# Two attention loops of an fp32 two-block transformer: copies moved from DVE to ACT, weight conversions behind head copies, and an output tile one turn earlier

## The reference

```python
h = rmsnorm(x, n1); proj = h @ w_in
qa = axial_rope(rmsnorm(qa, q_norm), ...); ka = axial_rope(rmsnorm(ka, k_norm), ...)
ya = global_gqa(qa, ka, va)                      # 8 query heads, 2 key heads
yb = dilated_window_attention(qb, kb, vb)        # 8 heads, partial rope
y = concatenate([rmsnorm(ya, out_norm_a), rmsnorm(yb, out_norm_b)])
x = x + y @ w_out
u = square(relu(rmsnorm(x, n2) @ w_mlp_in)); x = x + u @ w_mlp_out
```

## Time and profile before

| | |
|---|---|
| timed runs | 2024.04 us median of 3 (2023.94 to 2024.36) |
| profiled execution | 2016.69 us, of which span 2014.9 us |
| mean granted TensorE clock | 0.973 |
| TensorE busy | 1870.3 us, 93% |
| DVE, ACT, POOL busy | 72%, 55%, 18% |
| chain that ended last | TensorE 78%, DVE 10%, ACT 5%, issue 4% |

### The profile page before, as it was taken

One profiled execution on the slowest core, in us unless ns is written; L12 is line 12 of the kernel. 1 busy time (PEld: TensorE's weight loads), 2 busy tenths in 40 slices (PEclk: granted clock), 3 DMA queues, 4 the chain that ended last, 5 costly groups with the idle time before them and its releaser, 6 DMA issues.

```text
span 2014.9 us, 26999 instructions
## 1 busy us (share of the span) xinstructions
PE 1870.3 (93%) x9005; PEld 1519.5 (75%) x9005; DVE 1457.9 (72%) x1677; ACT 1117.0 (55%) x1355; POOL 353.2 (18%) x292
## 2 busy tenths in 40 slices
PE   6889999979999997899989779999999999999995
PEld 5677886857888675688877558888888888888884
DVE  5548874455876676544467668989898989898985
ACT  5644443554443454444345446767677777777773
POOL 2722203443100463200045300000000000000000
PEclk9999999989999998899999889999999999999998
DMA  8328983417986341455453329999999999999992
GB/s 257 105 105 324 350 339 134 146 45 269 356 330 247 108 145 42 146 187 187 137 190 130 126 74 342 366 332 366 332 367 329 367 329 367 330 361 336 358 364 100
DMA packets 316453, 494.79 MB, mean 246 GB/s; under 512 B 22984, under 2 KB 238240, under 8 KB 310240
## 3 DMA queue, kind: packets, MB, share of 16 engines
q1 hardware_dynamic: 307584, 493.44, 70.8%
q10 hardware_dynamic: 8480, 0.13, 0.3%
q0 software_dynamic: 320, 0.36, 0.2%
HBM read 492.77 MB, written 1.10 MB: 245 GB/s over the span
## 4 chain that ended last, share of the span: by engine, by line
PE 78%; DVE 10%; ACT 5%; issue 4%; POOL 1%; DMA 1%; DVEq 0%; SPq 0%; POOLq 0%; ACTq 0%
PE bank L2088 23%; PE bank L2090 23%; PE bank L2089 23%; ACT w_hi L1700 2%; PE bank L2202 2%; ACT slab L1847 2%; PE bank L2550 2%; DVE w_lo L876 1%; DVE slab L1181 1%; PE bank L2293 1%; PE bank L2271 1%; PE bank L2508 1%; POOL w_lo L774 1%; DMA slab<-in_w_in 1%; DVE big L1622 1%
## 5 line engine op out<-in xcount | busy, mean ns | idle before, releaser
L876 DVE TENSOR_TENSOR w_lo<-slab,w_hi 128x2048 fp32r<-128x2048 f32 x371 | 855.0, 2308 | 232.6 <-ACT w_hi L1700 232.6
L1700 ACT ACTIVATE w_hi<-slab 128x2048 fp32r<-128x2048 f32 (+2 forms) x421 | 796.9, 1899 | 361.4 <-PE bank L2090 272.9
L2088 PE MATMUL bank<-w_hi,hT_hi 128*128 128x512 f32 (+3 forms) x1616 | 632.8, 392 | 16.4 <-DVE hT_lo L925 4.3
L2090 PE MATMUL bank<-w_hi,hT_lo 128*128 128x512 f32 (+3 forms) x1616 | 619.2, 383 | 0.0
L2089 PE MATMUL bank<-w_lo,hT_hi 128*128 128x512 f32 (+3 forms) x1616 | 618.8, 383 | 0.0
L2088 PEld LDWEIGHTS bank<-w_hi,hT_hi 128*128 128x128 f32 x1616 | 306.2, 189 | 75.0 <-DVE w_lo L876 9.1
L2090 PEld LDWEIGHTS bank<-w_hi,hT_lo 128*128 128x128 f32 x1616 | 305.9, 189 | 57.9
L2089 PEld LDWEIGHTS bank<-w_lo,hT_hi 128*128 128x128 f32 x1616 | 306.7, 190 | 52.5
L774 POOL TENSOR_TENSOR w_lo<-slab,w_hi 128x512 fp32r<-128x512 f32 (+2 forms) x200 | 254.9, 1309 | 397.2 <-ACT w_hi L1700 397.2
L2088 PE MATMUL bank<-w_hi,hid_hi 128*128 128x512 f32 x728 | 285.0, 391 | 6.2 <-DVE hid_lo L1449 6.2
L2090 PE MATMUL bank<-w_hi,hid_lo 128*128 128x512 f32 x728 | 284.3, 391 | 0.0
(11 more groups left out here) (224 smaller groups left out, 1337.9 us busy)
## 6 DMA issues: line engine op xcount, KB each, us to landing
slab<-in_w_exp_gate SPq DMA_DIRECT2D x176, 512.0 KB, 5.3
slab<-in_w_exp_up SPq DMA_DIRECT2D x176, 512.0 KB, 6.3
slab<-in_w_exp_down SPq DMA_DIRECT2D x176, 512.0 KB, 5.9
slab<-in_w_ada SPq DMA_DIRECT2D x48, 1024.0 KB, 5.0
slab<-in_w_mlp_in SPq DMA_DIRECT2D x64, 512.0 KB, 6.2
slab<-in_w_mlp_out SPq DMA_DIRECT2D x64, 512.0 KB, 6.2
slab<-in_w_in SPq DMA_DIRECT2D x56, 512.0 KB, 5.0
slab<-in_w_out SPq DMA_DIRECT2D x32, 512.0 KB, 4.6
```

What stands on the lines that cost most here:

```text
L876: dve.tensor_tensor(w_lo[:, q, 0:n], raw(s)[:, 0:n], w_hi[:, q, 0:n].bitcast(F32), ALU.subtract).then_inc(lo_dve, 1)
L1700: act.activation(w_hi[:, q, 0:n], raw(s)[:, 0:n], ACT.Copy).then_inc(hi_done, 1)
L2088: pe.matmul(dst, a_hi, b_hi, start=start, stop=False)
L2090: return pe.matmul(dst, a_lo, b_hi, start=False, stop=stop_)
```

## The change

Four edits, all for the first block (`l < DEPTH`); the second block's layers run through the same helpers with their old order.

1. For pairs 2 to 7 `second_out` is no longer on DVE but on ACT, right behind `first_out` and ahead of `y_high`.
2. In ACT's turn 2 the head copies `turned_out(4, 5, 6)` come ahead of the high parts of tiles 11 and 12.
3. TensorE does the second output tile in turn 8, between `values(6)` and `values(7)`, after the last `mx_done`, and into the score banks 0 and 1 instead of the banks PT. The products of turn 9 and the sum of squares follow each other directly. `add_part(1)` reads the score banks.
4. In DVE's turn 8 `add_part(0)` comes after `y_low(6)` instead of ahead of it.

```diff
--- before.py
+++ after.py
@@ -479,6 +479,10 @@
 
         def dup(t, o):
             return h[:, t, o:o + HD]
+
+        def both_by_act(l, u):
+
+            return l < DEPTH and u >= 2
 
         def y_square(u):
 
@@ -1266,37 +1270,37 @@
                                           ).then_inc(ms_done, 1)
                         roots[0] += 1
 
-                    def scaled(c, t, o):
+                    def scaled(c, t, o, banks):
                         at = x[:, t, c * COL:(c + 1) * COL]
-                        return dve.scalar_tensor_tensor(at, bank[(FA, PT)[c][t]][:, :], stat[:, 2, o + t:o + t + 1], at,
+                        return dve.scalar_tensor_tensor(at, bank[banks[c][t]][:, :], stat[:, 2, o + t:o + t + 1], at,
                                                         ALU.mult, ALU.add)
 
                     def add_part(c):
                         dve.wait_ge(w_used, FREE_SPLIT + T0 + tiles_in(l) + c + 1)
                         for t in range(TT):
-                            scaled(c, t, 2).then_inc(xp_done, 1)
+                            scaled(c, t, 2, (FA, SC)).then_inc(xp_done, 1)
 
                     def add_last(c, t):
                         if c and not t:
                             dve.wait_ge(part_done, PARTS * l + 1)
                         else:
                             dve.wait_ge(w_used, FREE_SPLIT + T0 + tiles_in(l) + 3 + c)
-                        updated(scaled(c, t, 4))
+                        updated(scaled(c, t, 4, (FA, PT)))
 
                     for n in range(NU + 2):
                         if n < NU:
                             masked_max(n)
                         if n == 6:
                             part_mean(2)
-                        if 0 <= n - 1 < NU:
+                        if 0 <= n - 1 < NU and not both_by_act(l, n - 1):
                             second_out(n - 1)
-                        if n == 8:
-                            dve.wait_ge(rstd_done, roots[0])
-                            add_part(0)
                         if n < NU:
                             normalise(n)
                         if 0 <= n - 2 < NU:
                             y_low(n - 2)
+                        if n == 8:
+                            dve.wait_ge(rstd_done, roots[0])
+                            add_part(0)
                         if n == 0:
                             query_rows()
                         if n == 1:
@@ -1853,6 +1857,11 @@
                     act.wait_ge(av_done, U0 + u)
                     act.activation(pt_set(0), bank[PT[0]][:, :], ACT.Copy).then_inc(pta_done, 1)
 
+                def second_out(u):
+
+                    act.wait_ge(ptb_t, pairs_before(l, u) + 1)
+                    act.activation(pt_set(1), bank[PT[1]][:, :], ACT.Copy).then_inc(ptb_done, 1)
+
                 def y_high(u):
 
                     k, half_ = y_chunk(l, u), bank[OB][:, (u % 2) * SEQ:(u % 2 + 1) * SEQ]
@@ -1880,6 +1889,8 @@
                             soft_exp(n)
                         if 0 <= n - 1 < NU:
                             first_out(n - 1)
+                            if both_by_act(l, n - 1):
+                                second_out(n - 1)
                         if 0 <= n - 2 < NU:
                             y_high(n - 2)
                         if n == 0:
@@ -1890,9 +1901,8 @@
                             hi_of(l, 10)
                             empty(VB1, COL, FA, 9)
                         if n == 2:
-                            hi_of(l, 11)
                             turned_out(4, 5, 6)
-                            hi_of(l, 12)
+                            hi_of(l, 11, 12)
                         if n == 8:
                             hi()
                         if n == 9:
@@ -2221,7 +2231,7 @@
                     turn_rows(ATT2_BANKS)
 
                 def banks_of(two):
-                    return [bank[b] for b in two]
+                    return [bank[b] for b in two[:TT]]
 
                 def in_tile(i, to, waits_rows=False):
 
@@ -2375,9 +2385,9 @@
                             pe.wait_ge(yl_done, PAIR0[l] + B1)
                             pe.wait_ge(ms_done, ROOT0[l] + 4)
                             out_tile(0, FA, True, True)
-                        if n == 9:
-                            out_tile(1, PT, True, True)
-                    pe.wait_ge(mx_done, 4 * (U0 + NU))
+                        if n == 8:
+                            pe.wait_ge(mx_done, 4 * (U0 + NU))
+                            out_tile(1, SC, True, True)
                     squares_sum(B1, SC[2])
                     pe.wait_ge(yl_done, PAIR0[l] + NU)
                     pe.wait_ge(xp_done, 2 * TT * l + TT)
```

## The result

The kernel after took 2011.19 us (median of 4 runs, 2008.17 to 2012.67), the kernel before 2024.01 us (4 runs, 2023.94 to 2024.36): a ratio of 0.9939 [0.9924, 0.9954], so it is 12.8 us (0.6%) faster where I had forecast 6.2, and the time lies below my range. Two more comparisons of the same two kernels, each on one chip in turn, gave 0.9962 [0.9947, 0.9977] both times (2014.27 against 2022.16 and 2013.16 against 2021.42 us, medians), which is 7.7 and 8.0 us. So two things need an explanation: why the best measured difference is some 8 us and not 6.2, and why the first comparison showed 12.8.

What follows compares the result with a forecast made beforehand. TensorE, busy 93% of the span, was taken as the bound, losing time at waits in the attention loops. Terms -5.89 - 1.47 + 1.2 = -6.2 us took 2024.0 to 2017.8 us, range 2014.0 to 2022.5.

Steps and rivals of the forecast that it cites:

- Part 1: Attention loops' ends: second output tile one turn forward removes TensorE's 2.67 us wait; gains 3.75 and 2.14, together 5.89 us.
- Part 3: ACT's turn 2: head copies ahead of weight parts; TensorE's later wait costs clock, +1.2 us, bounds 0 and +2.4.
- A fall is gone at 87.44, where it cost nothing that ended last in layer 0: Half clock after TensorE's 4.69 us wait for the first heads disappears, claimed to save nothing in layer 0.
- the exponentials at 91.0: Layer 0: pair 3's exponentials start at 91.0 as before, since ACT's work changes order, not sum; a well earlier start refutes.
- Part 2: Second score copy from DVE to ACT, six pairs a layer: +0.13 us layer 0, -1.60 layer 1, sum -1.47.
- first rival: More half clock: wait before first sum of squares grows 1.54 to 2.0 us, layer 0 falls too; 2022.2 us, chance 0.24.
- third rival: Less half clock: other spacing spares layer 1's 6.8 us stretch; 2015.5 us, or 2014.3; chance 0.12.
- The wait that I had expected at 4.4 us: TensorE waits for pair 3's normalised scores, before the transposes at 95.5; a 2.03 us wait becomes 4.4.
- nothing comes of it: Attention's gain is given back where the DMA sets the pace; time stays 2024 us, chance 0.07.
- slower: Half clock falls on product tiles all over four layers' attention loops; 2028 us, chance 0.07.

Runs made afterwards that it cites:

- tile_only: Kernel before with only the second output tile moved between the products of pairs 6 and 7 (edits 3 and 4): 2017.34 us, ratio 0.9976.
- heads_only: Kernel before with only the head copies put ahead of the weights' high parts on ACT in turn 2: 2016.97 us, ratio 0.9969.
- fill_turn2: Kernel before with 24 unread transposes in TensorE's 4.7 us wait in turn 2, ACT's order unchanged: 2017.53 us, ratio 0.9979.
- heads_split: Changed kernel with ACT's turn 2 as one head copy, weight 11's high part, two head copies, weight 12's high part: 2014.57 us, ratio 0.9955.
- no_heads: Changed kernel with the old ACT order in turn 2, a weight's high part ahead of the head copies: 2016.73 us, ratio 0.9962.
- no_copies: Changed kernel with the second score copy back on DVE: 2013.49 us, ratio 0.9956.
- squares_nocopy: Changed kernel with the first sum of squares in turn 6, the split head copies, and the second score copy back on DVE: 2011.76 us, ratio 0.9950.
- squares_split: Changed kernel with the first sum of squares in turn 6 and the late head copies split by a weight conversion: 2009.74 us, ratio 0.9944.
- fill_turn5: Changed kernel with 12 unread transposes in TensorE's wait before the first sum of squares: 2011.52 us, ratio 0.9956.
- squares_late: Changed kernel with the first sum of squares moved on TensorE from the end of turn 5 into turn 6: 2011.2 us, ratio 0.9941.

## Why the prediction was wrong, and where it was right

**Part 1 was right about its own stretch.** Forecast -5.89 us; from the first output tile to the third it is -5.3 us in the kernel after and -5.6 in tile_only, the new wait 0.48 us for 0.46. Every kernel with this edit has 16.6 to 16.9 us there, those without it 18.4 to 20.2: that is shown, and it is the largest term of the loops' 7.9 us. What it brings the whole kernel when it stands alone is less (2.6 us in the loops, -4.6 +- 1.9 in the runs), and its new wait was priced without a clock: in layer 1 the third tile behind it starts at half clock, and its first nine matmuls take 3.5 us where they took 2.2, 1.3 us that the forecast has at nothing. The third tile starts at 130.99 and 451.18 us, forecast 130.7 and 452.6; but the first of these hits by luck, for the loop starts 0.8 us earlier than before and loses 3.0 us in pair 6.

**Part 3 is the step that failed**: a loss of 1.2 us was forecast; heads_only takes -5.0 +- 2.4 us, and pairs 3 and 4 are 3.65 us shorter in it. It failed with the sentences "this part moves TensorE's wait instead of removing it" and "A fall is gone at 87.44, where it cost nothing that ended last in layer 0", and with the exponentials at 91.0. The order of ACT in layer 0's turn 2 and 3:

```profile
84.10 1.08 ACT L1842 ACTIVATE slab<-bank 128x512 f32<-128x512 f32 x2
...
84.84 0.63 PE L2249 MATMUL bank<-const,h 128*128 128x128 f32 x4 [2.90 <-ACT slab L1842]
...
85.50 0.60 ACT L1842 ACTIVATE slab<-bank 128x512 f32<-128x512 f32 x1 [0.32 <-PE bank L2249]
...
86.00 3.70 ACT L1704 ACTIVATE w_hi<-slab 128x2048 fp32r<-128x2048 f32 x2
...
89.60 0.50 ACT L1851 ACTIVATE slab<-slab,att 128x256 f32<-128x256 f32 x1
```

From the start of the first item to the exponentials it is 5.50 us, before 6.12 (84.91 to 91.03). I had taken ACT's work as a fixed sum "with the same short wait for the heads inside it". That wait was not fixed: 0.78 us before, since TensorE did the head transposes at half clock behind a wait of 4.69 us, and 0.32 us behind one of 2.90. The rows of the kernel before that stand between those of the earlier trace rows, and DVE's first maximum of pair 3:

```profile
88.56 0.60 ACT L1838 ACTIVATE slab<-bank 128x512 f32<-128x512 f32 x1 [0.78 <-PE bank L2239]
...
89.06 1.90 ACT L1700 ACTIVATE w_hi<-slab 128x2048 fp32r<-128x2048 f32 x1
...
90.57 0.42 DVE L1164 CUSTOM_DVE_ANT_0 slab<-bank,const 128x256 f32<-128x256 f32 x1 [4.04 <-PE bank L2253]
```

The other 0.17 us: before, the exponentials (91.03) started 1.97 us after the last conversion did (89.06); in fill_turn2 it is 1.80 (88.04 to 89.84), and here two conversions take 3.60 to that point. So before they also waited 0.17 us for a late maximum, which waited for the scores (90.57) and ended at 90.99. Pair 4 shows the same (5.51 and 6.72 to 4.92 and 4.61). I had priced a fall of the clock as something that this part adds; it was already paid for before, and the part took its cost away. Which of two things takes it away does not matter: with the heads first TensorE goes on 1.8 us earlier, counted from the loop's start, and still falls to half clock right behind the transposes, in heads_only too:

```profile
85.30:88.70 3.40, 3.40 (x18) 2.34 (x16) 1.47 (x8) 3.40 (x3) 3.40 (x4) 0.50 0.52 193
```

With the filling it starts as late as before, at full clock, and the pairs are as quick. The rival theory, that the gain needs the new order itself, fell with fill_turn2. That ACT's own sequence holds pairs 3 and 4 once TensorE is not late is argued, not shown; heads_split, which takes the wait of 0.32 us out of that sequence, fits it with 8.11. What the gain is worth beside the other parts is open: pairs 3 and 4 are 2.3 us shorter in the kernel after than in no_heads, the loops 1.8, and the runs show nothing of it (-7.7 both).

**Part 2 was counted partly on the same lateness.** Forecast -1.47. Of its -1.60 us in layer 1, 1.15 were the lateness of pair 3 in the earlier trace rows, which is half clock behind that same wait; part 3 removes it without any copy. Alone the copies are worth 0.6 us in the loops and -3.1 +- 1.6 in the time. Beside the other parts they shorten the loops by 1.5 us (no_copies against after) and by 1.4 (squares_nocopy against squares_split), near the forecast but at other places than the two it names: 1.0 of the 1.5 lies ahead of the first output tile. The runs can't show it: no_copies -10.2 +- 2.2 against -7.7 and -8.0 for the whole change, squares_nocopy 1.2 +- 2.3 us slower than squares_split. What they are worth in time stays open.

**The first rival was right about its place and did not decide.** The wait before the first sum of squares grew to 2.02 us, and the clock fell in layer 0 too:

```profile
93.74 1.09 PE L2281 MATMUL bank<-const,slab 128*128 128x128 f32 x8 [2.48 <-DVE slab L1185]
...
102.12 0.36 ACT L1870 ACTIVATE big<-bank 128x256 f32<-128x256 f32 x1
...
102.54 3.57 PE L2314 MATMUL bank<-const,big 128*128 128x1 f32 x16 [2.02 <-ACT big L1870]
...
106.04 2.08 PE L2263 MATMUL bank<-slab 64*128 64x256 f32 x8
```

Sixteen matmuls of one column took 3.57 us instead of 1.95, the scores behind them 2.08 instead of 1.14, and pair 6 took 3.0 us more (9.49 for 6.45); I had said 3.2. But layer 1 got 1.0 of it back (7.17 for 8.13): half clock lies on 3.4 us there (426.80, window above) instead of 6.8. So the third rival, "less half clock", was half right as well. The wait that I had expected at 4.4 us (pair 3's transposes) is the 2.48 us ahead of 93.74 there, and full clock followed it (1.00 from 93.80). The Trainium skill ("TensorE: Matmul & The Clock Gate", HAM oscillation) tells of a kernel whose bursts of matmuls, with waits of some 3 to 5 us between them, start at half rate every time. The prediction left the length of those waits out. The waits here are shorter and have no one outcome: behind that of 2.02 us the clock was 0.50, behind that of 2.90 us the first transposes still ran at full clock (0.63 us) and half clock came after them, and behind that of 2.48 us it was 1.00. The rivals "nothing comes of it" and "slower" did not come: the kernel after's mean is below before's in all three comparisons.

**The size of the miss.** The loops gave 7.9 us. After them some is paid back: the kernel after has a half-clock stretch at 157.10 at the start of layer 0's feed-forward that before does not have (clock 0.50, window above), and the segments between the loops and from the second loop to layer 2's first exponential are about 1.0 and 0.5 us longer in its three profiles than in the two of before. The stretch at 157.10 need not be the cause of the 1.0: in fill_turn5 the clock is 1.00 there and the segment is as long (249.5 us, before 248.5). That leaves about 6.4, close to my forecast of 6.2, by luck, for it is reached by other terms. The runs of one chip say 8. The rest of the 12.8 is which runs were taken: in 92 runs the kernel before lies between 2014.9 and 2028.5 us with a mean of 2022.7, and the median of its first four was 1.3 above it; in 18 runs the kernel after lies between 2008.2 and 2020.8 with a mean of 2013.6, and the median of its first four was 2.4 below it. All runs pooled, over several chips, the difference is 9.1 +- 1.5 us (9.1 + 1.3 + 2.4 = 12.8), and 8.3 without the first comparison. The first four of the kernel before lie within 0.4 us of each other, though its 92 runs spread over 14 us; why is not known. In 87 runs of the kernel before for which both are known, time and mean granted clock go together (correlation -0.64). That scatter comes from where half clock falls in layers 2 and 3 is what the two profiles of before suggest, for 3.7 of their 6 us; that it explains the 12.8 us is argued, not shown. What stays open is the 1.3 to 2.7 us between the loops' account and the runs'; the way to the first loop, which the change doesn't touch, was 1.1 us shorter in the three profiles of after than in the two of before.

**A version that beats both.** squares_late takes -12.6 +- 2.2 us, against -7.7 +- 2.4 for the change itself on another chip, and its loops are 4.3 us shorter than after's (138.2 for 142.5). squares_split, measured beside the change on one chip, is 3.4 +- 2.4 us faster than it, and its loops are 4.1 us shorter. The wait ahead of the sum of squares was there in all versions that have the sum in turn 5, with the next pair's scores behind it. The sum slows at half clock by about the same factor as its neighbours (3.57 us for 1.95; scores 2.08 for 1.14): what was costly is its place, between a wait and those scores.

## What to carry to other kernels

Before a wait is called harmless, look at what the engine does in the first microseconds after it: here a wait of 4.7 us cost nothing by itself (the filled one is as long), and 2.3 to 3.7 us in two layers together through half clock behind it, by which kernels are compared. Work that needs something just made (the sum of squares) is moved to a place where its input is old, rather than the wait filled; a filling may only move the half clock elsewhere. Moving the sum moved half clock too, to where it cost less. And where the granted clock differs from run to run, four runs of each kernel give a ratio that is too sure of itself: divide the profile into segments, and run both kernels many times in turn.

## What the runs showed of the hardware

Three things I had not expected. Twenty-four transposes that nobody reads, put into a wait, make a kernel 4.3 +- 1.8 us faster, 2.0 of it in its two loops, and the transposes and scores behind that wait run at a granted clock of 1.00 instead of 0.51. The same wait is followed by either clock: 2.66 us by 1.00 in layer 1 before, 2.67 by 0.52 in layer 0; 2.48 by 1.00 and 2.02 by 0.50 in the kernel after. And two profiles of one kernel have all the distances in two loops equal to 0.1 us, while the clock over the first 25 us was 1.00 in one and 0.77 in the other.
